# Stationary blocks of the rows 192 and of the activation 96 bytes further modulo 256, and one small product behind the activation's second transposes

## The reference, cut to what matters

```python
logits = (x @ w_router) + b_router
top_v, top_e = lax.top_k(logits, 4)            # of 32 experts
gates = softmax(top_v)
# for the rows xb that are sent to expert e:
h = xb @ w_gate_up[e] + b_gate_up[e]           # 1024 -> 2048
gate = minimum(h[:, 0::2], 7.0)
up = clip(h[:, 1::2], -7.0, 7.0)
act = (up + 1.0) * gate * sigmoid(1.702 * gate)
y[rows] += gates * (act @ w_down[e] + b_down[e])   # 1024 -> 1024
```

## Time and profile before

| | us |
|---|---|
| median of 3 runs | 1380.27 |
| the profiled execution's own time | 1378.44 |
| its span, first to last instruction | 1376.7 |
| PE busy | 1347.8 (98%) |
| DVE busy | 1208.2 (88%) |
| ACT busy | 1090.7 (79%) |
| POOL busy | 993.9 (72%) |
| mean granted clock of TensorE | 0.993 |

### The profile page before, as it was taken

One profiled execution on the slowest core, in us unless ns is written; L12 is line 12 of the kernel. 1 busy time (PEld: TensorE's weight loads), 2 busy tenths in 40 slices (PEclk: granted clock), 3 DMA queues, 4 the chain that ended last, 5 costly groups with the idle time before them and its releaser, 6 DMA issues.

```text
span 1376.7 us, 19701 instructions
## 1 busy us (share of the span) xinstructions
PE 1347.8 (98%) x6762; PEld 997.0 (72%) x6762; DVE 1208.2 (88%) x1092; ACT 1090.7 (79%) x1149; POOL 993.9 (72%) x431
## 2 busy tenths in 40 slices
PE   8999999999999999999999999999999999999995
PEld 5988655667777777777777777777777777777773
DVE  5466555899999999999999999999999999999996
ACT  5354413788889888888888888888888888888885
POOL 2122212266699999999999898898888888989843
PEclk9999998999999999999999999999999999999998
DMA  9521271999999999999999999999999999999984
GB/s 354 192 67 67 94 275 70 354 395 371 368 351 376 369 378 383 386 383 388 372 388 395 368 390 371 385 374 383 381 391 375 383 386 379 385 377 386 382 313 151
DMA packets 51802, 458.99 MB, mean 333 GB/s; under 512 B 11449, under 2 KB 15515, under 8 KB 26121
## 3 DMA queue, kind: packets, MB, share of 16 engines
q1 hardware_dynamic: 40089, 438.33, 81.1%
q0 software_dynamic: 10000, 18.19, 6.0%
q10 hardware_dynamic: 1648, 1.65, 0.4%
HBM read 446.62 MB, written 22.08 MB: 340 GB/s over the span
## 4 chain that ended last, share of the span: by engine, by line
PE 70%; DVE 6%; POOL 3%; issue 2%; DMA 1%; ACT 1%; POOLq 0%; ACTq 0%; DVEq 0%
PE psum L2376 22%; PE psum L2375 22%; PE psum L2374 22%; DVE low L1693 4%; PE psum L2358 1%; PE psum L2369 1%; DMA area<-hn_tbl,idx_i 1%; POOL brow L671 1%; POOL slot_tbl L724 1%; PE psum L1913 1%; POOL small L813 0%; DVE area L1775 0%; DVE area L1778 0%; DVE area L1768 0%; DVE area_r L1757 0%
## 5 line engine op out<-in xcount | busy, mean ns | idle before, releaser
L1693 DVE TENSOR_TENSOR low<-raw,high 128x2048 fp32r<-128x2048 f32 x384 | 872.8, 2304 | 32.9 <-ACT high L1101 32.8
L1101 ACT CAST high<-raw 128x2048 fp32r<-128x2048 f32 x384 | 727.4, 1913 | 20.2 <-PE psum L2376 17.1
L2374 PE MATMUL psum<-high,area_r 128*104 128x512 f32 x1536 | 606.3, 395 | 3.2 <-DVE area_r L1757 1.5
L2376 PE MATMUL psum<-low,area_r 128*104 128x512 f32 x1536 | 602.1, 392 | 0.0
L2375 PE MATMUL psum<-high,area_r 128*104 128x512 f32 x1536 | 599.7, 390 | 0.0
L671 POOL PARTITION_BROADCAST brow<-brow x192 | 325.4, 1773 | 45.8 <-DMA brow<-in_biases 45.4
L2374 PEld LDWEIGHTS psum<-high,area_r 128*104 128x104 f32 x1536 | 257.8, 168 | 93.3 <-DVE low L1693 2.1
L2376 PEld LDWEIGHTS psum<-low,area_r 128*104 128x104 f32 x1536 | 257.0, 167 | 93.7
L2375 PEld LDWEIGHTS psum<-high,area_r 128*104 128x104 f32 x1536 | 258.2, 168 | 88.5
L668 POOL COPY arrived<-cst 1x1 f32 x60 | 227.6, 3793 | 15.1 <-DMA brow<-in_biases 14.8
L740 POOL DMA_INDIRECT area<-hn_tbl,idx_i x32 | 162.8, 5088 | 79.6 <-DVE idx_i L1660 40.5
(11 more groups left out here) (269 smaller groups left out, 1150.3 us busy)
## 6 DMA issues: line engine op xcount, KB each, us to landing
raw<-in_w_gate_up SPq DMA_DIRECT2D x128, 2048.0 KB, 12.9
raw<-in_w_down SPq DMA_DIRECT2D x64, 2048.0 KB, 13.2
ring<-in_w_in SPq DMA_DIRECT2D x7, 1024.0 KB, 15.2
ring<-in_x_prompt SPq DMA_DIRECT2D x8, 512.0 KB, 9.9
ring<-in_w_out SPq DMA_DIRECT2D x7, 512.0 KB, 4.5
ring<-in_w_mem_kv SPq DMA_DIRECT2D x2, 1024.0 KB, 9.2
ring<-in_mem_kT SPq DMA_DIRECT2D x1, 2048.0 KB, 8.8
ring<-in_cache_mem_v SPq DMA_DIRECT2D x1, 2048.0 KB, 8.2
```

What stands on the lines that cost most here:

```text
L1101: nc.scalar.copy(high_w(i), raw_w(t)).then_inc(sem("w_high"), 1)
L1693: v.tensor_tensor(low_w(t), raw_w(t), high_w(i), ALU.subtract).then_inc(sem("w_low"), 1)
L2374: mm(bank, high, wh, start=False, stop=False, skip_group_check=True)
L2376: return mm(bank, high, wl, start=False, stop=stop, skip_group_check=True)
```

## The change

Two new constants set by how many floats the views of the rows (`XO`) and of the activation (`AO`) are moved within `area_r`: 48 floats are 192 bytes, 24 floats are 96 bytes. The unused 24 floats at the end of `xL`'s last block make room for the second, so the blocks don't overlap. The buffers behind them (`gt`, `sg`, `up`, `yrow`, `hot`) move by 192 bytes. And `act_rows` gets a parameter `settle`: in each period but the last, PE issues one more float32 product behind the transposes of the second half, with the identity as both operands, 104 stationary columns and 8 (k = 0, 1) or 40 (k = 2 and above) moving ones, into columns of bank 6 that nothing reads. It is issued in 31 periods: 14 times with 8 columns and 17 times with 40.

```diff
 XS, AS = 128, 128
+XO, AO = 48, 24
...
         xg = moe_buf([2, D])
-        xH, xL = (view(area_r, a[0] + i * KD * XS, [KD, XS])[:, :, 0:CAP] for i in range(2))
-        a[0] += 2 * KD * XS
-        aH, aL = (view(area_r, a[0] + i * KD * AS, [KD, AS])[:, :, 0:CAP] for i in range(2))
+        xH, xL = (view(area_r, a[0] + XO + i * KD * XS, [KD, XS])[:, :, 0:CAP] for i in range(2))
+        a[0] += 2 * KD * XS + XO
+        aH, aL = (view(area_r, a[0] - XO + AO + i * KD * AS, [KD, AS])[:, :, 0:CAP] for i in range(2))
         a[0] += 2 * KD * AS
...
-            def act_rows(n, fh, overflow=False):
+            def act_rows(n, fh, overflow=False, settle=0):
...
                 last.then_inc(sem("act_pe"), 1)
+                if settle:
+                    mm(banks[6][0:CAP, 424:424 + settle], ident[:, 0:CAP], ident[:, 0:settle], start=True, stop=True, skip_group_check=True)
...
                     gate_up(n, 8, last, k + 1)
-                    act_rows(n, 1)
+                    act_rows(n, 1, settle=8 if k < 2 else 40)
                     gate_up(n, 9, last, k + 1)
```

## The result

| us | before | after |
|---|---|---|
| median of 6 runs each, same chip | 1381.01 (1379.94 to 1383.71) | 1392.22 (1391.83 to 1394.99) |
| ratio, 95% interval | | 1.0086 [1.0073, 1.0099] |
| span of the profiled execution | 1376.7 | 1390.2 |
| start of expert 9, of expert 31 | 568.45, 1325.69 | 571.70, 1339.04 |

The change makes the kernel 11 us slower, where 5 less were forecast. It is outside the range, which ended at 1384, and beyond the slower rival's 1388.9. From expert 9 to the end of expert 30 the periods repeat. These 22 periods take 757.24 us before and 767.34 after: 10.1 of the 13.5 us between the two spans arise there, 0.46 in each period. Another 2.6 arise in the same way from expert 2 to expert 8, whose start-up waits differ from run to run.

What follows compares the result with a forecast made beforehand. The prediction took PE to bound the kernel, with the transfers near their limit. Shorter steps, -7.8 us, and the small product, +2.8, summed to -5.0: 1380.3 to 1375.3 us, range 1370 to 1384.

Steps and rivals of the forecast that it cites:

- the slower rival: Experts' products: the new starts are worse, +1.25 ns a product, with the small product +8.6 us: 1388.9 us; chance 0.18.
- What bounds the kernel: PE, busy for all 34.42 us of a period, waits for nobody, so a step saved there shortens the span.
- The limit of the queue: Weight transfers: a gain up to about 10 us in total finds the weights there; more is cut off by the queue.
- I take half of the gain, -1.7 ns: Experts' 4608 products: moved starts shorten each step by half of the 3.3 ns read in `z_half`, -7.8 us.
- on the slow side: Rows of `z_half`: distance 0 modulo 256, where all experts' products stand, is the slow one, by 3.3 ns on each step.
- The bounds of 3.3 ns either way: Step of one experts' product: between -3.3 and +3.3 ns, ends of -15.2 and +15.2 us over the kernel.
- The strict transfer from half 1 of `z_half`: Rows' new distance of 64 is among those of half 1, worth 0.4 ns at most, -1.2 us.
- I take 0.09: Small product behind the last transpose: 0.09 us each, +2.8 us over 31; upper end 0.12 if 32 more columns come on top.
- 2 x 215: Float32 products of 512 columns: 430 ns each, only 3 ns above 2 x 213.3, so the excess belongs to the fp32r stream.
- The lower end: Small product: takes over the 0.07 us already spent on a late load and adds 0.02 each, +0.6 us in all.
- The other engines: ACT and DVE write the moved blocks by the same instructions at no cost, with 3.7 and 1.9 us of room a period.
- The rival stood at 1383.1 us: Experts' products: the starts change nothing and only the small product's 2.8 us is added; chance 0.27.

Runs made afterwards that it cites:

- e1: The change's moved starts of rows and activation without the small product, against the kernel before: 1386.3 us, ratio 1.0045.
- e3: Only the rows' blocks moved, by 192 bytes, no small product, against the kernel before: 1387.4 us in one execution.
- e4: Only the activation's blocks moved, by 96 bytes, no small product, against the kernel before: 1380.4 us in one execution.
- e15: The changed kernel with the small float32 product ahead of the second transposes instead of behind, with 80 columns: 1392.8 us in one execution.
- e2: The small product alone, with the blocks at their old starts, against the kernel before: 1385.1 us, ratio 1.0036.
- e17: The change's starts; small product replaced by an fp32r one of 4, 24, 44 or 64 columns ahead of the second transposes from expert 8: 1382.8 us, one execution.
- e9: The change's starts, no small product, second transposes moved ahead of half 8, to the switch between halves 7 and 8: 1387.8 us, ratio 1.0052.
- e5: The changed kernel with 16, 24, 32 and 48 columns in the small product by k: 1393.9 us in one execution.
- e6: The changed kernel with 56, 64, 72 and 80 columns in the small product by k: 1392.3 us in one execution.
- e11: The changed kernel with the small float32 product, 8 columns, ahead of the second transposes instead of behind: 1379.2 us in one execution.
- e10: Old starts, no small product, second transposes moved ahead of half 8, against the kernel before: 1383.0 us, ratio 1.002.
- e12: Old starts, small product behind the transposes with 32 stationary columns in place of 104: 1388.8 us in one execution.
- e14: Old starts, small float32 product ahead of the second transposes, against the kernel before: 1381.9 us in one execution.
- e18: The change's starts; small product replaced by an fp32r one of 24 columns ahead of the second transposes from period 8: 1380.3 us, 1.0002 of before.

## Why the prediction was wrong, step by step

**What bounds the kernel: right.** PE waits for nobody before and after, and what a period of PE grew by is what the kernel grew by: 22 x 0.46 = 10.1 of the 11 us. The limit of the queue never came in, since nothing was gained.

**"I take half of the gain, -1.7 ns": the step that failed.** Its size came from three steps of `z_half`, whose rounding alone was as large as what was read from them (in the finer times such triples at the one distance 0 take 0.376 to 0.390 us), and its sign from the thought that the present distance was "on the slow side". In e1 the moved blocks cost 0.23 us a period, **+1.6 ns** a product in the mean in place of -1.7: 7.4 us in place of a gain of 7.8, against the 6.9 measured. The gain's mechanism exists, and its size was about right: behind the transposes of `x_rows` the step is 226.7 ns, 2.1 less than 228.8. Wrong was the premise under it, that a start has a step: in the change the same blocks have a faster one and a slower one, and the slow one holds for at least 96 of the 144 products of a period. The bounds of 3.3 ns either way hold the fast step and the mean, but not the slow one (+4.5 ns).

**The slower rival: right in kind.** It ended at 1388.9 by 1.25 ns a product and a small product of 2.8 us; measured were 1.6 ns and 5.7 us. It had 0.18, because its evidence was called missing ("no row shows the distance 160"). It turned out that the distance of the rows, 64, is the costly one (e3), and that of the activation costs 0.03 us a period (e4). The strict transfer from half 1 of `z_half`, "worth 0.4 ns at most", failed with it.

**The small product: mis-sized.** "I take 0.09" stood for one record of the five in the earlier trace rows; those are products of the fast type, with one pass each. A float32 product has two, each with a load. The earlier trace rows could have told it: their eight records belong to four products, as `part` multiplies four tiles, so a product takes 2 x 430 ns, and both the prediction's "2 x 215" and its 0.84 ns a column are those of one pass (the two passes of 80 columns in e15 start 0.07 us apart). 2 x 0.09 = 0.18 fits the 0.18 us by which half 9 starts later in e2, and 0.02 for a slower restart of half 9 give its 0.21 us; the 32 columns more, which were the upper end, cost nothing. Over 31 periods, at e2's 4.5/22 each, that is 6.4 us (5.7 measured) where 2.8 stood, with an upper end of 3.3. The lower end, in which the product hides in the late load, didn't occur: the late load is still there behind it (981.88 to 982.18, 0.30 us).

**The other engines: right.** DVE's and ACT's writes at other starts cost nothing that shows (32.76 and 30.81 us of a period), and no engine is waited for. That a chunk's time to landing would rise above 14.0 us late in the run didn't come: it fell to 10.5, as no gain pressed the queue.

**What the forecast said would show it wrong** came as written in two cases: 84 products in 19.33 us where 19.10 was the slower case, and equal starts with different steps in different halves, "the start isn't the whole cause". The third, a small product that costs more "because the products behind it take up another rhythm", came for another reason: the rhythm behind is slow without it too (e1), and at the old starts it doesn't change with it (e2).

**The rule of the Trainium skill.** In the kernels e3 and e4 the same products read blocks of the same size from another start, and the step is 226.7 to 233.3 ns where it was 228.8. From the Trainium skill, "SBUF — State Buffer" (Who interferes with whom), by which TensorE never waits on anyone, and "TensorE: Matmul & The Clock Gate" (Part 2, Step-by-step), by which the next weights' load takes nothing from the running product, the prediction drew that a start can't matter. The measurement decides against that conclusion; whether the two reads get in each other's way, which these pages exclude, no run here shows. The rival stood at 1383.1 us with 0.27, and with the true price of the product it would have given 1386.

**What stays open** is what in PE or its reads makes the rhythms. The runs show that the stationary blocks' start sets which there are, and that a change of the entry as small as 20 columns, by which half 9 starts 0.002 us later (e17), brings another one, which lasts until the next transposes or, as in e3, until the blocks change. They don't show why, nor how to foretell it: both had to be measured. That it is the timing of the entry that picks is argued and not shown: no run changed the timing alone, and in e9 equal times of 0.530 us go ahead of both.

## What to carry to other kernels

Move the start of an operand only with the step read in every stretch between two interruptions, since a mean over the kernel hides that one half of it gained and the other lost; a start at which all stretches have one step is worth keeping. Count a small float32 product as two passes with a load each, check that a knob moves what it is meant to move before its result is read (the widths of e5 and e6 didn't move the entry), and take a price of three steps with two decimals for no more than a sign that is unknown. And a few microseconds gained on the engine that sets the pace have still to pass the end of the program, where a read that is timed by something else can take them back.

## What the runs showed of the hardware that wasn't expected

- Identical products with identical starts run at 226.7 ns in one stretch and at 232.0 or 233.3 in another, at a granted clock of 1.00 (after, e1, e11). In e3 a cycle of three periods runs over a loop of four. In e1 the slow stretches of two neighbouring periods take 19.25 and 19.33 us in turn.
- 64 columns in place of 44 ahead of the transposes, or 80 in place of 8, decide between them; the first product of the row starts 0.587 us after the last of the row before in place of 0.585, and 0.687 in place of 0.678 (e17; e15 against e11).
- Behind the transposes ten widths of a float32 product from 8 to 80 columns leave the next product's start at 0.71 to 0.72 us (after, e5, e6).
- With blocks at a distance of 0 modulo 256 bytes there was one rhythm, 228.8 ns, under every entry that was tried (before, e2, e10, e12, e14).
- A float32 product of 8 columns between other work costs 0.21 us behind the transposes and 0.15 ahead of them, one of 8 or 40 columns with 32 stationary columns 0.35, a one-pass product of 24 columns some 0.05 (e2, e14, e12, e18).
- A pause of PE of 3.5 us near the end was followed by 5.5 us at a granted clock of 0.51, the level of 1.2 GHz, in which a product's step was 427 ns in place of 227 (e18).
